# Stick-breaking attention: v of all heads projected first, then one unrolled pipeline over all score units with both heads issued together

## What is computed

```python
def sb_core(q, k, v, q_pos, k_pos):
    z = jnp.einsum('bqhd,bkhd->bhqk', q, k, preferred_element_type=jnp.float32) * SB_SCALE
    mask = k_pos[None, :] < q_pos[:, None]
    log_keep = jnp.where(mask, jax.nn.log_sigmoid(-z), 0.0)
    after = lax.cumsum(log_keep, axis=3, reverse=True) - log_keep
    w = jnp.where(mask, jnp.exp(jax.nn.log_sigmoid(z) + after), 0.0)
    return jnp.einsum('bhqk,bkhd->bqhd', w.astype(v.dtype), v)
...
def sb_qkv(x, w_in):
    B, S, _ = x.shape
    qkv = (x @ w_in).reshape(B, S, 3, N_HEADS, HEAD_DIM)
    return qkv[:, :, 0], qkv[:, :, 1], qkv[:, :, 2]
```

## Time and profile before

| | |
|---|---|
| time, median of 3 runs | 2860.22 us (2856.65 to 2865.72) |
| the profiled execution | 2856.74 us, its span 2855.0 us |
| TensorE busy | 2682.7 us of the span (94%), VectorE 1116.1, ScalarE 850.1 |
| the chain that ended last | TensorE 84%, VectorE 9%, ScalarE 3%, issue 2%, DMA 2% |
| mean granted TensorE clock | 0.966 of 2.4 GHz |
| HBM | 258.72 MB moved, 91 GB/s |

### The profile page before, as it was taken

One profiled execution on the slowest core, in us unless ns is written; L12 is line 12 of the kernel. 1 busy time (PEld: TensorE's weight loads), 2 busy tenths in 40 slices (PEclk: granted clock), 3 DMA queues, 4 the chain that ended last, 5 costly groups with the idle time before them and its releaser, 6 DMA issues.

```text
span 2855.0 us, 38995 instructions
## 1 busy us (share of the span) xinstructions
PE 2682.7 (94%) x16380; PEld 2369.8 (83%) x16380; DVE 1116.1 (39%) x1545; ACT 850.1 (30%) x1253; POOL 79.4 (3%) x174
## 2 busy tenths in 40 slices
PE   7999999799999998999999789988888899999997
PEld 7998998799899877998998666666665799899976
DVE  3323334633233356332333444444444543233265
ACT  3212222322122235321222243444444332122133
POOL 3000000100000000000000000000000000000000
PEclk9999999899999999999999899999999999999999
DMA  5213221332132222222322255555543332222130
GB/s 155 75 55 100 74 71 35 105 97 71 56 104 71 71 67 81 82 76 63 91 71 63 71 145 150 149 149 149 149 125 108 105 103 72 71 75 78 52 105 39
DMA packets 382955, 258.72 MB, mean 91 GB/s; under 512 B 10657, under 2 KB 347553, under 8 KB 382816
## 3 DMA queue, kind: packets, MB, share of 16 engines
q1 hardware_dynamic: 377616, 239.64, 28.6%
q0 software_dynamic: 5200, 17.04, 2.0%
HBM read 248.22 MB, written 8.42 MB: 90 GB/s over the span
## 4 chain that ended last, share of the span: by engine, by line
PE 84%; DVE 9%; ACT 3%; issue 2%; DMA 2%; DVEq 0%; SPq 0%; ACTq 0%
PE ps L1445 67%; PE ps L449 8%; PE ps L1453 6%; PE ps L510 2%; DMA raw<-in_ffn_w_dram 2%; DVE ring L1116 1%; DVE x L1165 1%; DVE s_sum L1261 1%; DVE x L1166 1%; PE ps L1507 1%; ACT x L899 1%; DVE stats L1126 1%; DVE xt_lo L1176 1%; ACT ring L886 1%; DVE e_buf L1224 1%
## 5 line engine op out<-in xcount | busy, mean ns | idle before, releaser
L1445 PE MATMUL ps<-xt_hi,ring 128*128 128x384 f32 (+1 forms) x5632 | 1230.7, 310 | 24.1 <-DVE xt_lo L1176 16.6
L1445 PEld LDWEIGHTS ps<-xt_hi,ring 128*128 128x128 f32 x5632 | 952.2, 190 | 27.1 <-DVE xt_lo L1176 18.2
L1445 PE MATMUL ps<-xt_lo,ring 128*128 128x256 f32 (+1 forms) x2816 | 871.5, 309 | 0.0
L1445 PE MATMUL ps<-ring,h_hi 128*128 128x512 f32 x1760 | 548.8, 391 | 0.0
L1445 PEld LDWEIGHTS ps<-xt_lo,ring 128*128 128x128 f32 x2816 | 536.4, 190 | 0.2
L886 ACT ACTIVATE ring<-raw 128x1024 fp32r<-128x1024 f32 (+1 forms) x302 | 300.5, 1027 | 454.2 <-PE ps L1445 364.5
L1116 DVE TENSOR_TENSOR ring<-raw,ring 128x1024 fp32r<-128x1024 f32 (+1 forms) x302 | 352.9, 1196 | 145.5 <-ACT ring L886 141.0
L1445 PEld LDWEIGHTS ps<-ring,h_hi 128*128 128x128 f32 x1760 | 332.1, 189 | 69.0
L1330 DVE SCALAR_TENSOR_TENSOR act<-act,ps 128x384 f32<-128x384 f32 (+1 forms) x176 | 85.8, 488 | 685.9 <-PE ps L1445 685.9
L1445 PE MATMUL ps<-ring,h_lo 128*128 128x512 f32 x880 | 343.7, 391 | 0.0
L1026 ACT ACTIVATE h_hi<-act 128x384 fp32r<-128x384 f32 (+1 forms) x176 | 82.8, 471 | 644.0 <-DVE act L1330 644.0
(11 more groups left out here) (143 smaller groups left out, 2147.9 us busy)
## 6 DMA issues: line engine op xcount, KB each, us to landing
raw<-in_ffn_w_dram SPq DMA_DIRECT2D x256, 512.0 KB, 4.4
k_raw<-in_cache_k_dram SPq DMA_DIRECT2D x128, 256.0 KB, 4.5
v_raw<-in_cache_v_dram SPq DMA_DIRECT2D x128, 256.0 KB, 4.5
raw<-in_ple_w_gate_dram SPq DMA_DIRECT2D x16, 512.0 KB, 4.2
a_raw<-in_sb_w_in_dram SPq DMA_DIRECT2D x16, 512.0 KB, 5.7
g_b<-in_ln_g_dram POOLq DMA_DIRECT2D x8, 512.0 KB, 4.1
b_b<-in_ln_b_dram POOLq DMA_DIRECT2D x8, 512.0 KB, 5.5
raw<-in_ffn_w_dram SPq DMA_DIRECT2D x16, 256.0 KB, 3.7
```

The source lines that it names most:

```text
L1445: return pe.matmul(out, w, xx, start=first, stop=last, skip_group_check=True)
```

## The change

- A new stage `v` before attention projects v for all heads at once with tokens on partitions (10 groups of 24 matmuls of 512 columns); ScalarE copies the groups into `v_tok`, which now holds all pairs and later also the attention output. POOL stores v from there. The transposes of v are gone, and so are the v projections inside the pairs. Its first two groups are followed by the transposes of x tiles 3 and 4.
- Weights of q and k go through the same ring and `cvt_to` as all others, in three slots; their projections are cut into 384 and 256 tokens (qA, qB, kA, kB).
- All engines run one unrolled program over 8 x 10 steps, with no boundary between pairs. Transposes of cached keys and all other uses of banks 6 and 7 are numbered events (`STEP_EVENTS`), two key blocks to a step; the bank of event n waits for the copy of event n-2. Projections of the next pair, key transposes to rows (kt4, kt1) and the transposes of past outputs are events too, issued at the end of a step.
- Scores and values of the two heads of a prompt part are issued together, alternating between the heads; the three masks of part 0 become one matmul of 384 columns for each head. Units are reordered so that both heads of a part are neighbours. A score step with two heads waits for the weights of a unit one later than before.
- The output is split into its parts during the last pair, and `out` begins in the steps behind the last pair with 7 of 8 chunks of its first four groups (`out_early`).

```diff
-UNITS = [("p", 0, 0), ("p", 1, 0), ("p", 0, 1), ("s", 0), ("p", 1, 1), ("s", 1), ("p", 0, 2), ("s", 2), ("p", 1, 2),
+
+UNITS = [("p", 0, 0), ("p", 1, 0), ("s", 0), ("p", 0, 1), ("p", 1, 1), ("s", 1), ("p", 0, 2), ("p", 1, 2), ("s", 2),
          ("s", 3)]
...
+STEP_EVENTS = {
+    0: [("kT", 0, 0), ("kT", 0, 1)],
+    1: [("kT", 0, 2), ("kT", 0, 3)],
+    2: [("tot",), ("qA",)],
+    3: [("kT", 1, 0), ("kT", 1, 1)],
+    4: [("kT", 1, 2), ("kT", 1, 3)],
+    5: [("past",), ("qB",)],
+    6: [("kT", 2, 0), ("kT", 2, 1)],
+    7: [("kT", 2, 2), ("kT", 2, 3), ("kA",)],
+    8: [("kT", 3, 0), ("kT", 3, 1), ("kB",), ("kT", 3, 2), ("kT", 3, 3)],
+    9: [("kt4",), ("kt1",)],
+}
+OF_NEXT = ("qA", "qB", "kA", "kB", "kt4", "kt1")
+ON_ACT = ("qA", "kA", "kB", "kt4")
...
+            def event_bank(key):
+
+                k = event_at[key][0]
+                if k >= 2:
+                    pe.wait_ge(*evacuated(event_order[k - 2]))
+                return 6 + k % 2
...
+            def scores(i, u):
+
+                g = NU * i + u
+                two = u in TWO_HEADS_AT
+                if g + two >= 4:
+                    pe.wait_ge(wt_done, g + two - 3)
...
+                    blocks = {0: [(4, 0), (3, P), (2, 2 * P)], 1: [(1, 0)], 2: [(0, 0)]}[part]
+                    for n, (kb, at) in enumerate(blocks):
+                        stop = TOKENS if kb == 4 else SEQ
                         for h in range(2):
                             rows = slice(HEAD_DIM * h, HEAD_DIM * (h + 1))
...
+                            mm(ps[:, (g + h) % 4, at:at + stop - kb * P], k_t[i % 2][rows, kb * P:(kb + 1) * P],
+                               q_t[i % 2][rows, kb * P:stop], start=n == 0)
+                    masks = mask_r[:, 0:3, :] if part == 0 else mask_r[:, 1:2, :]
+                    for h in range(2):
+                        ins = mm(ps[:, (g + h) % 4, 0:(3 if part == 0 else 1) * P], ident_r[:],
+                                 masks.rearrange("p m n -> p (m n)"))
+                    ins.then_inc(z_full, 2)
...
-                fill = {NU - 1: project_q, NU + 1: project_k}
-                for u in range(NU + 4):
-                    if u < NU:
-                        if u == 0:
-                            for which in range(2):
-                                pe.wait_ge(aux_free[which], AUX[which] * i + 2)
-                        scores(u)
-                    if u == 0:
-                        project_v(i)
-                        if begun:
-                            transpose_past(i - 1)
-                    if u == 1:
-                        to_tokens(i, k_t, 2)
-                    if u == 2:
-                        to_tokens(i, v_t, 3)
-                    if u + 1 in SAMPLE_AT:
-                        cached_keys(SAMPLE_AT.index(u + 1))
-                    if u == 3:
-                        own_totals()
-                    if 2 <= u < NU + 2:
-                        suffix(u - 2)
-                    if u == 5:
-                        first_values()
-                    if u >= 6:
-                        values(u - 4)
-                    if u in fill and not last:
...
+            for i in range(PAIRS + 1):
+                for u in range(NU if i < PAIRS else 5):
+                    events = events_of(i, u)
+                    if i < PAIRS and not (u and u - 1 in TWO_HEADS_AT):
+                        scores(i, u)
+                    late = [e for e in events if e[1][0] != "kT"]
+                    if u != 8:
+                        for owner, key in events:
+                            if key[0] == "kT":
+                                event(owner, key)
+                    else:
+                        for owner, key in events[0:2]:
+                            event(owner, key)
+                    behind = (i, u - 2) if u >= 2 else (i - 1, u - 2 + NU)
+                    if 0 <= behind[0] < PAIRS:
+                        suffix(*behind)
+                    if u == 2 and i < PAIRS:
+                        event(i, ("tot",))
+                    behind = (i, u - 4) if u >= 4 else (i - 1, u - 4 + NU)
+                    if 0 <= behind[0] < PAIRS and behind[1] not in TWO_HEADS_AT:
+                        values(*behind)
+                    for owner, key in late:
+                        if key[0] != "tot":
+                            event(owner, key)
+                    if u == 8:
+                        for owner, key in events[-2:]:
+                            if key[0] == "kT" and i < PAIRS:
+                                event(owner, key)
+                    if i == PAIRS and u < 4:
+                        out_early(u)
+            event(PAIRS - 1, ("past",))
...
+            load_keys(0)
+            load_unit(first_qk + QK_SLOTS)
+            for sample in range(4 * PAIRS):
+                i, su = divmod(sample, 4)
+                if sample + 1 < 4 * PAIRS:
+                    load_keys(sample + 1)
+                load_values(sample)
+                u = 2 * i + (4 if su == 0 else 5)
+                if su in (0, 2) and u < 2 * PAIRS:
+                    load_unit(first_qk + u)
+                if i == PAIRS - 1 and su == 0:
+                    for key in load_order[raw_at[first_out]:raw_at[first_out] + RAWS]:
...
+                for i in range(PAIRS + 1):
+                    for u in range(NU if i < PAIRS else 5):
+                        g = NU * i + u
+                        if i < PAIRS:
+                            exp_ln(g)
+                        for key in events_of(i, u):
+                            evacuate_event(key)
+                        before = (i, u - 1) if u else (i - 1, NU - 1)
+                        if 0 <= before[0] < PAIRS and UNITS[before[1]][0] == "s":
+                            sample_rows(*before)
+                        if 2 <= g < NU * PAIRS + 2:
+                            weights(g - 2)
...
+                        if i < PAIRS - 1 and u == 1:
+                            cvt_to(first_qk + 2 * i + 4)
+                        if i < PAIRS - 2 and u == 6:
+                            cvt_to(first_qk + 2 * i + 5)
+                        if i == PAIRS - 1 and u in (1, 2, 3):
+                            split_o(2 * u - 2)
+                            split_o(2 * u - 1)
+                        if i == PAIRS - 1 and u == 6:
+                            split_o(6)
+                            cvt_to(first_out + 3)
+                        if i == PAIRS and u == 0:
+                            cvt_to(first_out + 4)
...
+            def out_early(n):
+
+                pe.wait_ge(wt_done, NU * PAIRS - 3 + n)
+                for c in range(DC - 1):
+                    pe.wait_ge(o_lo_done, c + 1)
+                    if c % 2 == 0:
+                        split_of(out_stage.u0 + c // 2)
+                    token_major(n % 4, xt_hi, xt_lo, c, n, out_stage.u0 + c // 2, (c % 2) * DH, c == 0, False)
...
+                        if st.kind == "out" and n < 4:
+                            if n == 0:
+                                pe.wait_ge(o_lo_done, DC)
+                                split_of(st.u0 + 3)
+                            token_major(n % 4, x_hi, x_lo, DC - 1, t, st.u0 + 3, DH, False, True
+                                        ).then_inc(acc_full, 1)
+                            continue
...
+                if st.kind == "v":
+                    for n in range(2 * TILES):
+                        dh, t = divmod(n, TILES)
+                        if n >= 4:
+                            pe.wait_ge(v_done, n - 3)
+                        elif n < 2:
+                            pe.wait_ge(x_upd, st.y0 - 1 + n)
+                        if dh == 0:
+                            pe.wait_ge(piece_lo, prev.piece_at(t))
+                        for c in range(DC):
...
+                            ins = token_major(n % 4, xt_hi, xt_lo, c, t, u, (c % 2) * DH, c == 0, c == DC - 1)
+                            if t == TILES - 1 and c % 2 == 1 and c // 2 < 3:
+                                ins.then_inc(w_free, 1)
+                        ins.then_inc(v_full, 1)
+                        if n < 2:
+                            turn(prev, 3 + n)
```

914 lines of the change are left out of this document (437 added, 477 removed).

## The result

The changed kernel takes 2782.4 us (median of 4 runs, 2780.2 to 2791.1) where the kernel before takes 2858.4 in the same session: a ratio of 0.9737, 95% interval 0.9708 to 0.9767. It is 76 us faster; the forecast was 65. The profiled execution took 2782.0 us with a span of 2780.3. So a difference between two changed kernels is taken from their ratios, not from their medians.

The account below looks back on a forecast made before the run. TensorE was taken as the bound (84% of the chain, busy 94%). v stage, first projections, seven pairs of 62.2 us, last pair and tail end at 2179 against 2245: 65 us less, so 2795 us, range 2728 to 2850.

Parts of the forecast that it names:

- The v stage: Before attention: v projection starts at once, 54.5 us of matmuls plus two turns of x, 56.5 us, ending at 1646.
- first term: The v stage up to about 1646, said to be wrong if its 24-matmul groups show gaps or a late start.
- The first pair's projections: Behind the v stage: pair 0's projections alone 14.2 us, five transposes 0.7, three copies 1.8, ending at 1663.
- Work of a pair: TensorE's work in an attention pair: 67.5 us less 14.3 saved gives 53.2, low clock still included.
- The low clock's price: Attention pairs: about 3.8 us a pair lost at 1.2 GHz before, kept unchanged since gaps are as frequent.
- The waits of a pair: Seven TensorE waits walked through steps 1, 2, 3, 5, 7, 9 and 10 of a pair, 9.0 us in sum.
- The last pair: Pair without next projections or key transposes: 38.3 us of work plus 12 of waits, 50 us, ending at 2148.
- The part behind it: Last values, early and remaining out matmuls, and the fourth weight unit 5 us late: 31 us, ending at 2179.
- the waits are mostly covered: Rival on the pairs: waits of only 0 to 4 us a pair, 2720 to 2748 us; chance 0.20 (below 2762).
- The heads one after the other: Rival on scores: heads share no time, 2.3 us a pair, 18 in all, 2813; chance 0.15 including waits of 13 to 16.
- The slower case: Rival on the pairs: gaps in short work drop the clock; at about 0.80 the 65 us gain is gone; chance 0.10.

Follow-up runs that it names:

- e5: Changed kernel with the turns of x tiles 3 and 4 ahead of the first v group instead of behind its first two: 2793.1 us, ratio 0.9756.
- e3: Changed kernel with all four key blocks of sample groups 0 to 2 transposed and copied in one step instead of two: 2851.2 us, ratio 0.9961.
- e1: Changed kernel with a unit's score and mask matmuls issued for one head, then the other, instead of in turn: 2825.2 us, ratio 0.9866.
- e7: Changed kernel with the sums of own softplus rows behind the past values of step 2 instead of ahead: 2776.4 us, ratio 0.9705.
- e8: Changed kernel with the three edits of e2, e6 and e7 together: 2758.2 us, ratio 0.9640.
- e6: Changed kernel with a pair's second weight split one step later, on ScalarE and on VectorE: 2780.7 us, ratio 0.9715.
- e2: Changed kernel with ScalarE's unit weights and Exp of sample rows ahead of its copies of qA, kA, qB, kB and next keys: 2773.0 us, ratio 0.9694.

## Why the forecast was right, and where its steps were off

Against the forecast's clock times the changed stretch ended at 2172.5, not 2179. Term by term:

- **The v stage.** Right that it starts at once; by e5 that is worth 5 to 8 us. Work as forecast, but it ended at 1651.5, not 1646: TensorE waited 2.98 and 1.33 us for low parts of weights by VectorE and 0.69 for the last copy. The forecast asked whether x was ready and whether copies hide, and didn't walk the weights' split. By its own sign (no gaps to about 1646, or the first term is wrong) this term was wrong, by 5.5 us.
- **The first pair's projections.** 15.5 us, forecast 17.
- **Work of a pair.** Forecast 53.2, of which 3.7 for the low clock, so 49.5 at 2.4 GHz. Measured 49.37 at a clock of 1.00. Scores 4.0 us a pair (1.54, 1.12 and 1.34), forecast 3.95. The page that the forecast weighed (the Trainium skill, TensorEngine Tiling (Array Packing), Key Properties: tiles work in parallel) holds for two heads that split the rows: their four scores take 1.06 us, two of one head 1.05.
- **The low clock's price.** The step "I keep the low clock's price, since gaps are as frequent" was mis-sized: 3.7 us was kept, and 0 to 1.6 was paid. Neither frequency nor sum is the measure: the changed kernel's pairs wait more than those of before (9.7 us against 7.6) and lose less. Nor is length alone. In e3's first seven pairs every bunch ran slow, behind waits of 2.1 to 4.3 us; but in the kernel before, a wait of 1.69 us was followed by slow work too (the row below, the same eight transposes that take 1.06 us at full clock), while of the changed kernel's five waits of 1.99 us before kA three were followed by full speed, and e1 fell to 0.92 with no wait above 2.0. What sets the clock's price stays open. The work of the seven pairs came out 26 us under the forecast by it (346.3 instead of 372) and their waits 6 over (68.7 instead of 63): 20 us less in all (415.1 instead of 435).

```profile
1807.38 1.97 PE L510 MATMUL ps<-ident,k_raw 128*128 128x128 f32 x8 [1.69 <-ACT kc_t L934]
```

- **The waits of a pair.** Forecast 9.0, measured 9.69, and wait by wait: 1.3 / 1.38, 1.4 / 1.12, 1.2 / 1.07, 0.7 / 0.97, 1.8 / 1.99, 0.8 / 0.88, 1.8 / 1.64 (forecast / measured), with one of 0.44 that was missed.
- **The last pair.** 50.85 us with 12.1 of waits; forecast 50 with 12.
- **The part behind it.** 39.6 us, forecast 31. The 5 us for the late weight unit came as forecast (5.05). Missing were 3.65 us of waits (1.27 for sample rows, 2.38 for the low part of the last chunk) and 4.9 us because this work ran at a clock of 0.87.

The errors are +5.5, -1.5, -20, +0.9 and +8.6: -6.5. That the sum came out so close is partly luck: three terms were 15 us too small together and two 21.5 us too large. The rest of the program was 2.2 us shorter, for no reason that I looked for.

Of the rivals, "the waits are mostly covered" rested on the claim that lost and waiting time aren't additive. A pair waits 9.69 us at a clock of 1.00 and 9.68 at 0.97, so here they are: its slow spell is at kA's matmuls, behind the wait of 1.99. In e1, where the spell comes ahead of a wait, they are so only in part. "The heads one after the other" was priced at 18 us, 2.3 a pair; e1 says 33 in the pairs (448.4 against 415.1): the scores cost 3.0 a pair, the masks 0.5, and the clock comes on top. The slower case asked for a clock of 0.80 and had 0.99; its mechanism is real, as e3 shows with 4.2 us a pair at 0.93, and e1 too at 0.95, but this kernel's order hardly meets it.

By the experiments three parts of the change are worth 5 to 8 us (the turns of x behind the first v groups), 37 (both heads' scores in turn) and 64 (keys spread). That is more than the 76 us in all: each was taken out of the finished kernel, where a bunch of key turns waits longer than in the kernel before, and in e1 and e3 part of the loss is clock. Not tried by themselves: v of all heads in a stage of its own (7.1 us of projection and 0.66 of transposes less a pair, for 56.5 once), the values of both heads together, and "next q" earlier in the pair.

## What to carry to other kernels

When a pipeline's engines are all below half busy and TensorE still waits, walk the in-order queues of the copying engines: name for each wait the instruction that stands ahead in the queue, and ask which of these nobody waits for. Here three such reorderings, one later split and one earlier load took the ratio from 0.9737 to 0.9532, 59 us more, without touching the work. Price a wait of several microseconds at up to twice its length (e3: 5.0 us of waits cost 9.2 us a pair), because the work behind it may run at half clock.

## What the runs showed of the hardware that I had not expected

- Two pairs of one execution with the same waits took 59.05 and 60.65 us, in turn: a spell of low clock of 1.6 us in some, none in others. Of the six pairs behind the first, two had one in the changed kernel, none in e7 and e8, one in e6, but two in e2, whose waits are shorter than e7's. In the changed kernel it starts 0.8 us behind the wait of 1.99 us before kA, and the same wait stands in the pairs without it. What sets it off I can't say.
- The price of a wait through the clock can be as large as the wait: 5.0 us of added waits in e3 brought 4.2 us of slower work.
- Between executions the v stage began anywhere from 1589.5 to 1596.0 us in the profiles of kernels whose code up to there is the same. That is the noise that a comparison of single spans carries, and the reason why the periods of pairs were used.
